# First pair of heads and last two output tiles: another order, a third bank for V, VectorE shares the scaling of h

## The reference

```
h = RMSNorm(x) * g_mix;  one product h @ w_in gives all q, k, v and gates
A = stick-breaking attention, 8 heads of 64, q and k normalised per head
B = retention in chunks of 128 tokens, 8 heads (64 for q and k, 128 for v), rotary q and k,
    per-head RMSNorm, times silu(gate)
x += (sigmoid(gA) * (A @ w_a) + sigmoid(gB) * (B @ w_b)) @ w_out
h = RMSNorm(x);  x += (gelu(causal_conv3(h @ w_gate)) * (h @ w_val)) @ w_down
x += sigmoid(RMSNorm(x) @ w_pg) * (p @ w_pp)
```

## Time and profile before

| | us |
|---|---|
| median of 3 runs (range) | 888.08 (888.02 to 888.16) |
| time of the profiled execution | 888.43 |
| its span, first to last instruction | 886.6 |
| PE busy | 880.3 |
| DVE busy | 567.9 |
| ACT busy | 427.3 |
| POOL busy | 16.5 |

### The profile page before, as it was taken

How to read it: one execution, slowest core, us unless ns; L and a number is a source line. 1 busy time by engine, 2 the same in 40 slices (tenths; PEclk the granted TensorE clock), 3 DMA queues, 4 the chain that set the end, 5 groups by cost and what they waited for, 6 DMA issues and landing times.

```text
span 886.6 us, 12137 instructions
## 1 busy us (share of the span) xinstructions
PE 880.3 (99%) x4378; PEld 745.5 (84%) x4378; DVE 567.9 (64%) x737; ACT 427.3 (48%) x569; POOL 16.5 (2%) x19
## 2 busy tenths in 40 slices
PE   9999999999999999999999999999999999999998
PEld 6788888898898889999888888888888888888886
DVE  7898796796796887766556655566665542424444
ACT  7866866766765744434345333333333332323431
POOL 1500000000000000000000000000000000000000
PEclk9999999999999999999999999999999999999999
DMA  8224233233232133226323223222222323332241
GB/s 281 84 81 145 72 100 115 71 102 111 71 108 83 66 117 93 93 84 234 111 95 119 95 95 97 100 99 102 100 95 95 90 83 99 96 91 93 66 148 66
DMA packets 29824, 91.86 MB, mean 104 GB/s; under 512 B 4161, under 2 KB 5457, under 8 KB 29665
## 3 DMA queue, kind: packets, MB, share of 16 engines
q1 hardware_dynamic: 28496, 87.70, 30.6%
q10 hardware_dynamic: 1072, 3.67, 1.3%
q0 software_dynamic: 224, 0.06, 0.1%
HBM read 84.34 MB, written 2.10 MB: 97 GB/s over the span
## 4 chain that ended last, share of the span: by engine, by line
PE 97%; DMA 1%; DVE 1%; ACT 1%; issue 0%; SPq 0%; DVEq 0%
PE dense L502 28%; PE dense L503 28%; PE dense L504 28%; PE z L575 2%; PE aty L503 1%; PE aty L504 1%; PE aty L502 1%; PE z L504 1%; PE z L503 1%; PE z L502 1%; PE aty L607 1%; DMA fs<-in_xT 1%; PE aty L624 1%; PE aty L622 1%; ACT fs L893 0%; DVE fs L1437 0%
## 5 line engine op out<-in xcount | busy, mean ns | idle before, releaser
L502 PE MATMUL dense<-hi,w_hi 128*128 128x512 f32 x1038 | 407.3, 392 | 0.5 <-DVE fs L1440 0.3
L503 PE MATMUL dense<-lo,w_hi 128*128 128x512 f32 x1038 | 404.4, 390 | 0.0
L504 PE MATMUL dense<-hi,w_lo 128*128 128x512 f32 x1038 | 404.2, 389 | 0.0
L1437 DVE TENSOR_TENSOR w_lo<-w_f,w_hi 128x1024 fp32r<-128x1024 f32 (+2 forms) x156 | 177.8, 1142 | 159.2 <-ACT w_hi L908 155.2
L502 PEld LDWEIGHTS dense<-hi,w_hi 128*128 128x128 f32 x1038 | 195.0, 188 | 42.0 <-issue 1.1
L504 PEld LDWEIGHTS dense<-hi,w_lo 128*128 128x128 f32 x1038 | 194.9, 188 | 40.8
L503 PEld LDWEIGHTS dense<-lo,w_hi 128*128 128x128 f32 x1038 | 195.1, 188 | 38.4 <-issue 0.2
L908 ACT CAST w_hi<-w_f 128x1024 fp32r<-128x1024 f32 (+2 forms) x144 | 141.5, 983 | 113.0 <-PE dense L504 110.8
L1437 DVE TENSOR_TENSOR fs<-fs 128x512 f32<-128x512 f32 (+3 forms) x124 | 93.4, 759 | 3.4 <-ACT fs L893 0.2
L893 ACT ACTIVATE fs<-fs 128x512 f32<-128x512 f32 (+2 forms) x85 | 59.7, 707 | 52.7 <-DVE fs L1440 38.6
L1437 DVE TENSOR_TENSOR lo<-fs,hi 128x512 f32 (+3 forms) x59 | 47.4, 807 | 25.3 <-ACT hi L1370 20.2
(11 more groups left out here) (151 smaller groups left out, 812.6 us busy)
## 6 DMA issues: line engine op xcount, KB each, us to landing
w_f<-in_w_in SPq DMA_DIRECT2D x52, 512.0 KB, 3.4
w_f<-in_w_up SPq DMA_DIRECT2D x44, 512.0 KB, 3.2
w_f<-in_w_down SPq DMA_DIRECT2D x16, 512.0 KB, 3.5
w_f<-in_w_b SPq DMA_DIRECT2D x8, 512.0 KB, 3.3
w_f<-in_w_out SPq DMA_DIRECT2D x8, 512.0 KB, 3.5
w_f<-in_w_pg SPq DMA_DIRECT2D x8, 512.0 KB, 3.3
w_f<-in_w_down SPq DMA_DIRECT2D x8, 384.0 KB, 3.1
fs<-in_xT SPq DMA_DIRECT2D x4, 512.0 KB, 7.3
```

The source lines that it names most:

```text
L502: mm(out, w1, x1, start=start, stop=False, skip_group_check=skip)
L503: mm(out, w1, x0, start=False, stop=False, skip_group_check=skip)
L504: return mm(out, w0, x1, start=False, stop=stop, skip_group_check=skip)
L1437: return nc.vector.tensor_tensor(out, a, b, op).then_inc(done, 1)
```

## The change

Start and first pair, ACT: `first_exp(0)` comes before `first_log(1)`; the exponential that makes `A_RS` comes after both `high_qk`. In `first_back` the order behind `sb_high(0, 2)` is another, with `silu(0)` ahead of `y_move(0, 0)`.

V: `turn_v` of the first pair writes `ybank` instead of `misc`; `sb_turn(0, 0)` waits for two logarithms (`s_misc`) and no longer for `low_v(0)`.

h: DVE multiplies the first four tiles of `H_ORDER` (0, 1, 2, 4) by `A_RS` at the end of its `start`; POOL waits for them and does the other four (3, 5, 6, 7).

DVE's order in `first_back` is another. SP's part of the first pair is unchanged. At the end, the short product of tile 6 is cut into halves too, in `z[:, 0]` and `z[:, 1]`; its first half is a hook in the gate chunk of tile 7, and DVE and SP follow.

```
@@ pool
             pool.wait_ge(s_xrs, 1)
-            pool.wait_ge(s_raw_done, 2)
-            for n in H_ORDER:
+            pool.wait_ge(s_hd, H_DVE)
+            for n in H_ORDER[H_DVE:]:
@@ pe turn_v, sb_turn
-                    ins = nc.tensor.transpose(aty[:, 0, i * P:(i + 1) * P],
+                    ins = nc.tensor.transpose(v_bank(j)[:, i * P:(i + 1) * P],
...
                 if g == 0:
-                    pe.wait_ge(s_raw_done, RAWS * j + 3)
                     if not isinstance(j, int):
-                        pe.wait_ge(s_misc, 3 * j + 2)
+                        pe.wait_ge(s_raw_done, RAWS * j + 3)
+                    pe.wait_ge(s_misc, 3 * j + 2)
@@ pe, end
+            ple_tile(ple_place(KD - 2)[0], ple_place(KD - 2)[0], KD, T_H)
+            ple_tile(ple_place(KD - 1)[0], ple_place(KD - 1)[0], KD, T_H, hooks={4: lambda: half_tile(KD - 2, 0)})
+            half_tile(KD - 2, 1)
+            half_tile(KD - 1, 0)
+            half_tile(KD - 1, 1)
@@ act start
                 first_log(0)
-                act.wait_ge(s_xln, 1)
-                run(fs[:, A_RS, :], fs[:, A_RS, :], ACT.Exp, s_xrs, scale=-0.5)
+                first_exp(0)
                 first_log(1)
-                first_exp(0)
                 first_exp(1)
                 high_qk(0, 0)
                 high_qk(0, 1)
+                act.wait_ge(s_xln, 1)
+                run(fs[:, A_RS, :], fs[:, A_RS, :], ACT.Exp, s_xrs, scale=-0.5)
                 sigmoid_tables()
@@ act first_back
                 sb_high(0, 2)
                 high_h(6)
+                zero_half(T_RE)
                 y_out(0, 0)
                 high_h(7)
-                zero_half(T_RE)
-                zero_half(T_SBE)
-                high_rot(0, 0)
+                silu(0)
                 y_move(0, 0)
                 y_out(0, 1)
+                high_rot(0, 0)
+                zero_half(T_SBE)
                 ahead(0, 7)
-                silu(0)
                 high_rot(0, 1)
@@ dve start
                 evac_x(2)
+                for n in H_ORDER[:H_DVE]:
+                    x = fs[:, A_X + n, :]
+                    tt(x, x, fs[:, A_RS, :], ALU.mult, s_hd)
                 dve.wait_ge(s_rope, 16)
@@ dve first_back
                 sb_weights(0, 0)
+                ahead(0, 3)
                 low_v(0)
-                ahead(0, 3)
-                low_h(0)
                 sb_low(0, 0)
                 sb_weights(0, 1)
+                low_h(0)
                 ahead(0, 4)
                 low_h(1)
                 evac_x(3)
-                evac_x(4)
                 sb_low(0, 1)
                 sb_weights(0, 2)
                 ahead(0, 5)
+                evac_x(4)
+                sb_low(0, 2)
+                ahead(0, 6)
+                evac_x(5)
                 low_h(2)
                 low_h(4)
-                ahead(0, 6)
-                sb_low(0, 2)
-                evac_x(5)
+                evac_x(6)
                 low_h(3)
                 low_h(5)
+                rotate(0, 0)
+                rotate_sum(0, 0)
+                decayed(0, 0)
                 low_h(6)
-                turned(0, 0)
+                low_h(7)
+                rotate(0, 1)
+                rotate_sum(0, 1)
+                decayed(0, 1)
                 low_rot(0, 0)
-                low_h(7)
-                evac_x(6)
-                turned(0, 1)
                 ahead(0, 7)
                 low_rot(0, 1)
@@ dve, end
+            ple_out_half(KD - 2, 0)
             ple_gate(KD - 1)
-            ple_out(KD - 2)
-            ple_last()
+            ple_out_half(KD - 2, 1)
+            ple_out_half(KD - 1, 0)
+            ple_out_half(KD - 1, 1)
```

More of the change, by code:

```diff
@@ L81 @@
 N_F32 = 18
+H_DVE = 4
 H_ORDER = (0, 1, 2, 4, 3, 5, 6, 7)
@@ L133, in build @@
         s_xhi, s_xlo, s_xacc = sem("s_xhi"), sem("s_xlo"), sem("s_xacc")
+        s_half, s_halfm = sem("s_half"), sem("s_halfm")
+        s_hd = sem("s_hd")
         s_xln, s_xrs, s_hf, s_hhi, s_h = sem("s_xln"), sem("s_xrs"), sem("s_hf"), sem("s_hhi"), sem("s_h")
@@ L292, in sb_v, with v_bank, v_turned @@
             return (hi if hd == 0 else lo)[:, T_SBV, :].rearrange("p (b t d) -> p b t d", b=NT, t=2)
-        def v_turned(hd):
-            return misc.rearrange("p (b h d) -> p b h d", b=NT, h=2)[:, :, hd, :]
+        def v_bank(j):
+            return ybank if isinstance(j, int) else misc
+        def v_turned(j, hd):
+            return v_bank(j).rearrange("p (b h d) -> p b h d", b=NT, h=2)[:, :, hd, :]
         def quarter(t, row, col):
@@ L342, in norm_y_pair, with half_bank @@
             return fs[:, A_SQY:A_SQY + 5:4, :]
+        def half_bank(m, half):
+            return (z if m == KD - 2 else aty)[:, (0 if m == KD - 2 else 1) + half, 0:SEQ // 2]
         block = ctx.enter_context(nc.Block())
@@ L472, in _ @@
             load_pp(7)
-            for m in range(3, KD - 1):
+            for m in range(3, KD - 2):
                 store(m)
+            sp.wait_ge(s_y, KD)
+            sp.dma_start(outT[KD - 2], fs[:, A_X + KD - 2, :]).then_inc(s_out, 16)
             for half in range(2):
                 cols = slice(half * SEQ // 2, (half + 1) * SEQ // 2)
-                sp.wait_ge(s_y, KD + half)
+                sp.wait_ge(s_y, KD + 1 + half)
                 sp.dma_start(outT[KD - 1][:, cols], fs[:, A_X + KD - 1, cols]).then_inc(s_out, 16)
@@ L876, in _, with half_tile @@
                 ple_tile(at, at, KD if at % 2 == 0 else PB, T_H if at % 2 == 0 else T_P)
[L877 to L882, removed]
+            def half_tile(m, half):
+                at = ple_place(m)[1]
                 cols = slice(half * SEQ // 2, (half + 1) * SEQ // 2)
+                pe.wait_ge(s_wlo, PLE0 + at + 1)
                 for k in range(PB):
-                    ins = split3(aty[:, 1 + half, 0:SEQ // 2], w_hi[at % 3][:, k, :], w_lo[at % 3][:, k, :],
+                    ins = split3(half_bank(m, half), w_hi[at % 3][:, k, :], w_lo[at % 3][:, k, :],
                                  hi[:, T_P + k, cols], lo[:, T_P + k, cols], start=(k == 0), stop=(k == PB - 1))
-                ins.then_inc(s_used, 1)
+                ins.then_inc(s_half, 1)
+            ple_tile(ple_place(KD - 2)[0], ple_place(KD - 2)[0], KD, T_H)
[3 more added lines that the diff above has]
+            half_tile(KD - 1, 1)
         @block.scalar
@@ L1009, in high_v @@
                 for hd in range(2):
-                    ins = nc.scalar.copy(sb_v(hd)[:, :, 0, :], v_turned(hd))
+                    ins = nc.scalar.copy(sb_v(hd)[:, :, 0, :], v_turned(j, hd))
                 ins.then_inc(s_vhi, 1)
@@ L1111, in start @@
                 high_qk(0, 1)
+                act.wait_ge(s_xln, 1)
+                run(fs[:, A_RS, :], fs[:, A_RS, :], ACT.Exp, s_xrs, scale=-0.5)
                 sigmoid_tables()
             def high_h(k):
-                act.wait_ge(s_hf, H_ORDER.index(k) + 1)
+                n = H_ORDER.index(k)
+                act.wait_ge(*((s_hd, n + 1) if n < H_DVE else (s_hf, n + 1 - H_DVE)))
                 nc.scalar.activation(hi[:, T_H + k, :], fs[:, A_X + k, :], ACT.Identity,
@@ L1611, in low_v @@
                 for hd in range(2):
-                    ins = nc.vector.tensor_tensor(sb_v(hd)[:, :, 1, :], v_turned(hd), sb_v(hd)[:, :, 0, :],
+                    ins = nc.vector.tensor_tensor(sb_v(hd)[:, :, 1, :], v_turned(j, hd), sb_v(hd)[:, :, 0, :],
                                                   ALU.subtract)
@@ L2086, in ple_out, with ple_out_half @@
                 tt(x, x, t, ALU.add, s_y)
[L2088 to L2097, removed]
+            def ple_out_half(m, half):
+                n = 2 * (m - (KD - 2)) + half + 1
+                cols = slice(half * SEQ // 2, (half + 1) * SEQ // 2)
+                x, t = fs[:, A_X + m, cols], ple_gate_row(m)[:, cols]
+                dve.wait_ge(s_pg, m + 1)
+                dve.wait_ge(s_half, n)
+                tt(t, half_bank(m, half), t, ALU.mult, s_halfm)
+                dve.wait_ge(s_halfm, n)
+                tt(x, x, t, ALU.add, s_y)
             residual(7, 1, G_PLE, PLE0, (DOWN0 + 7) % 3)
```

## The result

The changed kernel takes 891.34 us (median of 7 runs, 890.12 to 892.44), against 888.11 (888.02 to 888.16) before: 1.0037 times as long, 95% interval 1.0025 to 1.0049. It is 3.2 us slower, not 1.4. The runs of before agree within 0.14; those of the changed kernel spread over 2.3. One of the seven kept a mean granted clock of 1.000 and took 890.12; the other six show means of 0.996 to 0.998 and take 891.3 to 892.4. Only one of them, the profiled execution, has a trace.

The account below looks back on a forecast made before the run. PE was taken to bound the kernel (busy 880.3 of 886.6 us). Span 886.6 + 1.86 (first pair) - 0.47 (end) = 887.99, plus 1.83 for the profiled execution, less 0.35 for the median: 889.5 us; range 886.7 to 890.6.

Parts of the forecast that it names:

- The clock: Granted clock, 1.000 throughout the earlier profile; the main case has it stay there, a fall being only the third rival.
- The sum: Whole kernel: span 886.6 + 1.86 - 0.47 = 887.99, giving a median of 889.5 us.
- third rival: PE's idle 2.9 before chunk 9 halves the clock for 6.4 us, costing 3.2: 892.7 us; chance 0.06.
- The swap: First pair: SP's first swap waits for a `low_h(4)` 2.39 later, so the pair ends 1.86 later.
- Two pieces of `low_rot`: DVE, first pair: `low_rot(0, 0)` now stands before `ahead(0, 7)` and takes 1.30 to the next start.
- no longer last: First pair: `low_rot(0, 1)`, at 72.28 to 73.67, no longer sets the start of `r_scores(0, 0)` at 73.95.
- V in the third bank: First pair: PE's transposes wait only for the first group's product, in time for 37.20; 0.45 back.
- four tiles on DVE: DVE before the first scan: four multiplications take 2.5 of 2.88 idle; cost nothing, margin 0.4.
- q normed first: Start of the first pair: DVE norms q sooner, so PE goes on at 27.41 instead of 27.68, 0.27 sooner.
- The end: Behind PE's last instruction: DVE's six half instructions end at 884.01, 0.47 sooner; bounds 0.3 and 0.6.
- signs of being wrong: PE standing under 1 us between 66 and 75, the swap issuing before 56, or a clock under 1.00.

Follow-up runs that it names:

- a3: Changed kernel plus 12 unused 512-column multiplications on PE between `r_v` and chunk 9: 890.03 us, 1.95 more than the kernel before.
- a1: Changed kernel with `low_h(2)` and `low_h(4)` right behind `ahead(0, 5)` on DVE, as before: 887.58 us, ratio 0.9994 to the kernel before.
- a2: Kernel before with only `low_h(2)` and `low_h(4)` moved behind `evac_x(5)` on DVE: 889.68 us, ratio 1.0018.
- b1: a1 with POOL starting its four tiles only after DVE's product of the first group: 887.64 us, ratio 0.9992 to the kernel before.
- c3: c2 plus V in the third bank (`turn_v`, `sb_turn`, `high_v`, `low_v` as changed): 888.15 us, ratio 0.9998 to the kernel before.
- c2: Kernel before with only ACT's new order in `start`: 888.11 us against 888.46 or 888.48 for the kernel before; ratio 0.9996.
- a4: Kernel before with only the change of the end (tile 6 in column halves on PE, DVE and SP): 887.65 us, ratio 0.9995.
- b4: Changed kernel with `ahead(0, 7)` moved in front of `rotate(0, 1)` on DVE: 893.37 us, 4.9 more than the kernel before.
- c1: Changed kernel plus 5 unused 512-column multiplications on PE between `r_v` and chunk 9: 890.37 us, 1.89 more than the kernel before.

## Why the prediction was wrong

**The clock** is the step that failed. The sum has no term for it. I had it as the third rival, with its place (PE's idle time before chunk 9) and a chance of 0.06, since "PE works densely on both sides, and that 0.28 to 0.31 of idle left the clock at 1.000". That was no evidence for a gap ten times as long, and PE's standing still ahead of the warm-up spoke the other way. In the trace the clock is at 0.50 for 3.41 behind a gap of 2.97, and six runs of seven have the means and the times of such a fall. a3 shows it as the cause of 1.3 at the median. Without it the time is 890.0 to 890.1, inside my range, 0.6 above the forecast of 889.5.

Its price was mis-sized too. I let the lower level last for the whole warm-up (6.4, for 3.2 us); it costs 1.3 at the median and 2.4 in the slowest run (892.44 against 890.03). The row of the warm-up didn't give the 6.4 either: its multiplications take 0.63 only until 6.6, some 5.1, and the last six take 0.40.

The traces have a sign that I didn't look at. At the end, where PE stops for good, the granted clock falls as well. In the trace before, this comes 4.5 behind PE's last instruction, which alone would not have decided a gap of 3. Over all thirteen traces it comes 2.1 (a1) to 4.5 behind it, so in a gap of 3 the clock may fall or stay.

**The swap** was right as a mechanism and nearly as a size. Forecast and measured: `low_h(4)` ends at 57.00 and 57.06, SP issues at 57.11 and 57.17, rotations start at 61.1 and 61.28, 67.05 and 67.16, w_lo is ready at 72.36 and 72.59, chunk 9 starts at 72.42 and 72.64, `r_scores` at 73.95 and 74.35. a1 and a2 show the cause from both sides. The trace of the changed kernel begins 0.18 earlier than that of before (w_lo at 25.27 and 25.45), so `r_scores` is in truth 0.6 late. That is the 0.6 by which the time without a fall still lies above the forecast. Three terms make most of it. Two pieces of `low_rot` were taken as 1.30; they take 1.41, and 1.42 in the trace before (70.35 to 71.77). `low_rot(0, 1)` was to be "no longer last"; it was. It ends at 74.01 in

```profile
73.32 0.69 DVE L1586 TENSOR_TENSOR lo<-fs,lo 64x512 fp32r<-64x512 f32 x1
```

and `r_scores` starts 0.34 behind that. Before it started 0.35 behind 71.74. In a3, at the full clock, `low_rot(0, 1)` ends at 73.93, and

```profile
74.27 0.73 PE L588 MATMUL z<-hi 128*128 128x512 f32 x2
```

comes 0.34 behind it, so the clock has no part in this. The third term is the next point.

**V in the third bank and four tiles on DVE.** I gave 0.45 back at the transposes and said that the product ends "between 36.4 and 37.3", against PE's 37.20, and took it as in time. It took 2.23, where I allowed "at most some 2.1", and ended at 37.25; PE's own pace would have given 36.97, and it started at 37.40, 0.43 late. Four tiles on DVE let POOL start a new instruction just before the product. This loss was not swallowed by the later wait: the second scans, from which DVE's queue runs almost without a pause to `low_h(4)`, start later by it. In b1 without it the scans start 0.48 earlier than in a1 (41.03 against 41.51), and so does the swap (53.57 against 54.05). And c3 shows that the bank's 0.45 isn't PE's to keep while DVE's scans come no sooner.

**q normed first**: 27.68 became 27.21, of which 0.18 is the earlier trace; 0.29 against 0.27. The trace agrees; the time (c2, 0.37 less) can't be told from it.

**The end**: 0.47 forecast, 0.43 measured (a4).

Of my signs of being wrong, one came: the clock shows less than 1.00. The others, on PE's wait, its place, the swaps and the end, came out as forecast.

## What to carry to other kernels

When an order is changed by hand, list for every instruction that moves the semaphore counts that another queue waits for. Here a DMA queue counted the fourth of eight, and two instructions moved past four others cost over 3 us through two transfers of 4 us each. When a change makes PE stand for some microseconds at full load (2.97 here), add the clock to the price and expect a spread. If the wait can't be removed, unused multiplications in its place take the clock's part back (1.3 us here). And work that is moved onto another engine's idle time decides what its partner then collides with.

## What the hardware showed that I had not expected

The clock doesn't fall at a fixed point of a gap. In the trace of the changed kernel it fell 4.4 after PE had stopped (69.67 to 74.05), which was 1.4 after PE had taken up work again; in b4 it fell 2.0 after PE had stopped (71.58 to 73.56), inside the gap. It stayed low for 3.41 and for 6.83. The same kernel kept a mean of 1.000 in one run of seven, with a gap of 2.97, and in one of five with 3.4 (b4). With a gap of 1.80 two runs of seven have the mean of a fall (c1, not traced), with 1.42 none of eleven (a2), and with the gap filled none of eleven (a3).

The granted clock of the view is no reading in the first microseconds: it shows 1.00 over the warm-up, where most multiplications take 0.63, as they do at 0.50 in the changed kernel.

Beside POOL, two VectorE instructions in a row took 2.23 and 2.29 instead of 1.22, because each had to wait for the end of a POOL instruction that was already running; where VectorE began first (b1), POOL's waited instead.
